# Hybrid RG-LRU / GLA step on one core: the first shift joined in behind the first projections, gates moved behind the second key, values' weights by column tiles

## The reference, cut to what matters

```python
mod = silu(c) @ ada_w + ada_b          # for each of the two conditions; six parts of 1024
shift1, scale1, gate1, shift2, scale2, gate2 = split(mod, 6)
h = rmsnorm(x, norm1_g) * (1 + scale1) + shift1
z = h @ w_in
xl, yl, q, k, v, og, gdn = split(z, (512, 512, 256, 256, 512, 512, 32))
xc = conv4(xl)                          # along the tokens, rows of 64 on the grid
# RG-LRU in both directions over xc, with gates from xc @ lru_wr, xc @ lru_wi (blocks of 64)
lru_out = gelu(yl) * (h_f + h_b)
glog = log_sigmoid(gdn @ gla_wg + gla_bg) / 16
# GLA in both directions, 4 heads, chunks of 64, cumulated glog in exponentials with q and k
x = x + gate1 * (concat(lru_out, norm(o) * silu(og)) @ w_out)
x = x + gate2 * moe(rmsnorm(x, norm2_g) * (1 + scale2) + shift2)     # 16 experts, 2 for each token
```

## Time and profile before

| what | value |
|---|---|
| median of 3 runs | 659.17 us (659.15 to 662.01) |
| profiled execution | 657.16 us, span 655.4 us |
| mean granted clock of TensorE | 0.943 |
| TensorE matmul busy | 572.9 us (87%) |
| VectorE, ScalarE, GpSimd busy | 242.9, 172.9, 51.4 us |
| moved by DMA | 131.42 MB, mean 201 GB/s |

### The profile page before, as it was taken

One profiled execution on the slowest core, in us unless ns is written; L12 is line 12 of the kernel. 1 busy time (PEld: TensorE's weight loads), 2 busy tenths in 40 slices (PEclk: granted clock), 3 DMA queues, 4 the chain that ended last, 5 costly groups with the idle time before them and its releaser, 6 DMA issues.

```text
span 655.4 us, 6115 instructions
## 1 busy us (share of the span) xinstructions
PE 572.9 (87%) x2354; PEld 304.5 (46%) x2354; DVE 242.9 (37%) x501; ACT 172.9 (26%) x314; POOL 51.4 (8%) x67
## 2 busy tenths in 40 slices
PE   2479989999969999999999999589999999999514
PEld 0145545544335556566545555535444454544201
DVE  0342438502951754111336665432112121211067
ACT  0630275638241220442311112010111101011122
POOL 3000000000060220000000000110001010100050
PEclk9789998999969999999999999588999999999957
DMA  9976245049533931500039000399999999972193
GB/s 326 392 241 193 61 148 205 1 133 348 192 128 81 358 89 40 176 1 1 1 109 392 31 14 33 121 378 341 382 365 368 372 359 381 352 265 96 66 343 137
DMA packets 76351, 131.42 MB, mean 201 GB/s; under 512 B 8137, under 2 KB 31010, under 8 KB 76322
## 3 DMA queue, kind: packets, MB, share of 16 engines
q1 hardware_dynamic: 70136, 108.96, 48.0%
q0 software_dynamic: 3744, 13.63, 5.5%
q10 hardware_dynamic: 2442, 8.43, 3.2%
HBM read 112.36 MB, written 18.65 MB: 200 GB/s over the span
## 4 chain that ended last, share of the span: by engine, by line
PE 55%; DVE 6%; ACT 2%; issue 1%; DMA 1%; POOL 1%; POOLq 0%; DVEq 0%; ACTq 0%
PE ms L1267 17%; PE ps L1201 11%; PE ps L1288 8%; PE ps L956 8%; PE ps L1250 2%; PE ps L1137 1%; PE ms L1172 1%; PE ps L1342 1%; DMA wring<-expert_rows,yidx 1%; PE ps L1127 1%; POOL wring L666 1%; PE ps L1086 1%; DVE tmp L1551 1%; PE ms L1240 1%; DVE tmp L1521 1%
## 5 line engine op out<-in xcount | busy, mean ns | idle before, releaser
L956 PE MATMUL ps<-r,wring 128*128 128x512 f32 (+1 forms) x512 | 143.9, 440 | 4.9 <-ACT gd L806 2.4
L956 PEld LDWEIGHTS ps<-r,wring 128*128 128x128 f32 x512 | 79.2, 192 | 69.1 <-issue 66.6
L1201 PE MATMUL ps<-wring,mixT 128*128 128x512 f32 x160 | 72.1, 599 | 0.5 <-DVE tmp L1640 0.5
L1267 PE MATMUL ms<-wring,tmp 128*128 128x512 f32 x128 | 58.8, 603 | 1.3 <-DVE tmp L1799 1.3
L1201 PEld LDWEIGHTS ps<-wring,mixT 128*128 128x128 f32 x160 | 29.2, 190 | 32.0 <-issue 31.3
L639 POOL DMA_INDIRECT mixT<-h_rows,slot_tok x16 | 15.3, 953 | 320.2 <-DVE slot_tok L1739 181.0
L1813 DVE COPY gd<-ps 128x256 f32<-128x256 f32 x16 | 6.8, 425 | 89.9 <-PE ps L1277 89.9
L972 PE MATMUL ps<-wring,cs 128*32 128x512 f32 x192 | 27.5, 719 | 12.9 <-DMA wring<-in_ada_w_dram 7.3
L904 ACT ACTIVATE tmp<-ms 128x256 f32<-128x256 f32 x16 | 6.1, 384 | 123.4 <-PE ms L1267 123.4
L1020 PE MATMUL ps<-wring,r 128*128 128x512 f32 x80 | 37.3, 623 | 1.4 <-ACT vtok L763 1.4
L1267 PEld LDWEIGHTS ms<-wring,tmp 128*128 128x128 f32 x128 | 24.2, 195 | 28.6 <-issue 27.0
(11 more groups left out here) (280 smaller groups left out, 716.6 us busy)
## 6 DMA issues: line engine op xcount, KB each, us to landing
wring<-in_ada_w_dram SPq DMA_DIRECT2D x12, 2048.0 KB, 12.9
wring<-in_exp_w_dram SPq DMA_DIRECT2D x8, 2048.0 KB, 13.6
r<-in_exp_w_dram SPq DMA_DIRECT2D x4, 2048.0 KB, 14.0
wring<-in_exp_w_dram SPq DMA_DIRECT2D x8, 1024.0 KB, 6.7
tmp<-in_exp_w_dram SPq DMA_DIRECT2D x4, 2048.0 KB, 14.3
expert_rows<-tmp ACTq DMA_DIRECT2D x16, 512.0 KB, 7.4
wring<-in_w_in_dram SPq DMA_DIRECT2D x12, 512.0 KB, 4.1
expert_rows<-zero SPq DMA_DIRECT2D x9, 512.0 KB
```

The costliest lines, as they stand in the source:

```text
L956: i = mm(d, lhsT, r, start=first, stop=last)
L1201: i = mm(product(f"mx{t}")[:, half * 512:(half + 1) * 512], mixT[:, k, t * P:(t + 1) * P], w[:, k, :], start=(k == 0), stop=(k == KD - 1))
L1267: i = mm(ms[:, b, :], xgT[:, b, k, :], e13[u % 4][:, k, :], start=(k == 0), stop=(k == KD - 1))
```

## The change

1. The first scales alone, from a2 and a3, now make `hT`; the shift is left out there. a2 and a3 and the xl weights are loaded ahead of a0 and a1, the small inputs and the rows of x ahead of all. The start's transposes stand among the products, and half of the scales (`first_scale`) is made from a2, half from a3.
2. a0 and a1 are multiplied behind xl0. Their sum with the bias is put into `shc` (128 x 8 x 32, in `gd`), a further product `adx` multiplies the xl weights with it, and its turned result `xb` is the bias that the shift brings to xl. ScalarE adds it to xl0 and xl1 in place (`bias_xl`) and to xl2 and xl3 as it takes them. Once xl3 is made, ScalarE and VectorE add the shift to `hT` in place (`shift_rows`), and gd waits for both.
3. The gates of chunks 2 and 3 stand right behind k1 and ahead of q0 on TensorE, and on ScalarE with their decays and roots ahead of the copies of q. Some turns and reductions of modulations stand later.
4. The weights of v are loaded in four tiles, each when the product of q or k that read those columns is made. a0 and a3 change slots, and so do the pieces behind them.

```diff
-        order = []
-        for j in range(4):
-            order += [(f"ad{j}", "A")] + [(f"aT{j - 1}", "D")] * (j > 0)
-        order += [("aT3", "D")]
-        order += [(f"xT{k}", "AD"[k % 2]) for k in range(KD)]
+        order = [("ad2", "A"), ("xT0", "A"), ("aT2", "D"), ("xT1", "D"), ("ad3", "A"), ("xT2", "A"), ("xT3", "D"), ("aT3", "D")]
+        order += [(f"xT{k}", "AD"[k % 2]) for k in range(4, KD)]
+        order += [("xl0", "A"), ("ad0", "A"), ("ad1", "A"), ("aT0", "D"), ("xl1", "A"), ("aT1", "D"), ("adx", "A"), ("xl2", "A"), ("aTx", "D")]
...
-        tiled = {"qk": ([f"xl{i}" for i in range(4)], 0), "og": (["v4"] * 4, 1), "yl": ([f"og{i}" for i in range(4)], 2)}
+        tiled = {"qk": (["adx", "adx", "xl2", "xl3"], 0), "v": (["q0", "q1", "k0", "k1"], 1), "og": (["v4"] * 4, 2),
+                 "yl": ([f"og{i}" for i in range(4)], 3)}
...
+            def bias_xl(t):
+                grid, rest = xl_parts(t)
+                act.wait_ge(took["A"], count(f"xl{t}")[1])
+                A(grid, grid, ACT.Identity, bias=xb[:, t, 0:1])
+                A(rest, rest, ACT.Identity, bias=xb[:, t, 1:2]).then_inc(xl_biased, 1)
+
+            def shift_rows():
+
+                act.wait_ge(shift_ready, 1)
+                act.wait_ge(product_ready, made["xl3"])
+                for k in range(0, KD, 2):
+                    A(hT[:, k, 0:NS], hT[:, k, 0:NS], ACT.Identity, bias=mod[:, k, 0:1])
+                    i = A(hT[:, k, NS:N], hT[:, k, NS:N], ACT.Identity, bias=mod[:, k, 1:2])
+                i.then_inc(hT_ready, 1)
...
             take_gates(1)
+            shift_rows()
+            take_mod(4)
+            take_mod(5)
             decays(0)
-            A(gd[:, :], ready("gd")[:, 0:N], ACT.Copy).then_inc(took["A"], 1)
...
             wait_piece(pe, "xl")
-            for t in range(3):
-                project(f"xl{t}", weights("xl"), t * P)
+            project("xl0", weights("xl"), 0)
+            two_of(modulation, 0)
+            project("xl1", weights("xl"), P, range(0, KD // 2))
+            two_of(turn_modulation, 0)
+            project("xl1", weights("xl"), P, range(KD // 2, KD))
+            modulation("x")
+            project("xl2", weights("xl"), 2 * P, range(0, KD // 2))
+            turn_modulation("x")
+            project("xl2", weights("xl"), 2 * P, range(KD // 2, KD))
...
             pe.wait_ge(gdw_in, 16)
+            pe.wait_ge(hT_ready, 2)
             dst = start("gd")
...
             project("k1", weights("qk"), QK + P)
+
+            for ch in (2, 3):
+                gates(ch, 0)
+                gates(ch, 1)
             wait_tile(pe, "qk", 0)
             project("q0", weights("qk"), 0)
             wait_tile(pe, "qk", 1)
             project("q1", weights("qk"), P)
             two_of(modulation, 6)
-            gates(2, 0)
+            for i in range(4):
+                wait_tile(pe, "v", i)
+            values(0)
             two_of(turn_modulation, 6)
-            gates(2, 1)
-            gates(3, 0)
-            gates(3, 1)
-            wait_piece(pe, "v")
-            values(0)
             values(1)
...
+            def first_scale(j):
+
+                a = 4 * (j - 2)
+                take_mod(j)
+                add_bias(KD + a, KD + a + 4)
+                for s in range(2):
+                    i = stt(A1[:, a:a + 4, s], mod[:, KD + a:KD + a + 4, s], 1.0, smT[:, N1 + a:N1 + a + 4], ALU.add, ALU.mult)
...
+            def shift_rows():
+                dve.wait_ge(product_ready, made["xl3"])
+                for k in range(1, KD, 2):
+                    ts_(hT[:, k, 0:NS], hT[:, k, 0:NS], mod[:, k, 0:1], None, ALU.add)
+                    i = ts_(hT[:, k, NS:N], hT[:, k, NS:N], mod[:, k, 1:2], None, ALU.add)
+                i.then_inc(hT_ready, 1)
...
             gate_input(1)
+            shift_rows()
+            recur(0)
             take_mod(4)
             take_mod(5)
-            recur(0)
             cumulate()
-            take_mod(6)
-            take_mod(7)
             gate_input(2)
```

More of the change, by code:

```diff
@@ L246, in turned @@
             return [(f"aT{j}", "D") for j in js]
-        order += [("xl0", "A"), ("xl1", "A"), ("xl2", "A")] + gates_order(0) + [("xl3", "A")] + gates_order(1)
-        order += adaln(4, 5) + [("gd", "A")] + turned(4, 5) + [("k0", "A")]
-        order += [(f"g{g}", "A") for g in range(4)] + [("k1", "A"), ("q0", "A")]
-        order += [("q1", "A")] + adaln(6, 7) + gates_order(2)[0:2] + turned(6, 7) + gates_order(2)[2:4] + gates_order(3)
-        order += [("v0", "A"), ("v1", "A")] + adaln(8, 9)
+        order += gates_order(0) + [("xl3", "A")] + gates_order(1)
+        order += adaln(4, 5) + [("gd", "A"), ("k0", "A")]
+        order += [(f"g{g}", "A") for g in range(4)] + turned(4, 5) + [("k1", "A")] + gates_order(2) + gates_order(3)
+        order += [("q0", "A"), ("q1", "A")] + adaln(6, 7)
+        order += [("v0", "A")] + turned(6, 7) + [("v1", "A")] + adaln(8, 9)
         order += [("v2", "A")] + turned(8, 9) + [("v3", "A")] + adaln(10, 11) + [("v4", "A")] + turned(10, 11)
@@ L268, in hybrid_step @@
                 made[name] = place[f"og{g}"] + n + 1
+        for n, name in enumerate(("aT0", "aT1", "xl1", "adx", "aTx", "xl2")):
+            made[name] = place["aT0"] + n + 1
         RING = 3
@@ L479, in _ @@
                                      blocks[half]).then_inc(lruw_in, 16)
+            load_piece("a4")
             load_piece("a5")
@@ L696, in take_mod @@
             def take_mod(j):
-                if j >= 2:
-                    act.wait_ge(product_ready, made[f"aT{j - 2}"])
-                A(adrow[j % 2], ready(f"ad{j}")[:, 0:512], ACT.Copy).then_inc(took["A"], 1)
-            take_mod(0)
-            take_mod(1)
+                n = modulations.index(j)
+                if n >= 2:
+                    act.wait_ge(product_ready, made[f"aT{modulations[n - 2]}"])
+                A(adrow[n % 2], ready(f"ad{j}")[:, 0:512], ACT.Copy).then_inc(took["A"], 1)
             for t in range(NT):
@@ L710, in _, with take_xT @@
             A(st[:, 2, :], st[:, 0, :], ACT.Sqrt, bias=eps[:, 0:1], scale=1 / D).then_inc(roots, 1)
+            def take_xT(k):
+                src = ready(f"xT{k}")
+                A(hT[:, k, 0:NS], src[:, 0:NS], ACT.Identity, bias=zero[:, 0:1], scale=A1[:, k, 0:1])
+                A(hT[:, k, NS:N], src[:, NS:N], ACT.Identity, bias=zero[:, 0:1], scale=A1[:, k, 1:2]).then_inc(took["A"], 1)
+            take_mod(2)
+            act.wait_ge(mod_out, 1)
+            take_xT(0)
+            take_mod(3)
+            take_xT(2)
+            act.wait_ge(mod_out, 2)
+            take_xT(4)
+            take_xT(6)
             chain(A(lam[:, 0, :], smT[:, LAM:LAM + 8], ACT.Abs))
@@ L986, in _, with turn_input @@
             pe.wait_ge(cs_ready, 1)
-            for j in range(4):
-                modulation(j)
-                if j:
-                    turn_modulation(j - 1)
-            turn_modulation(3)
-            pe.wait_ge(xhat_ready, 1)
-            for k in range(KD):
+            def turn_input(k):
+                pe.wait_ge(xhat_ready, 1)
                 dst = start(f"xT{k}")
@@ L997, in _ @@
                 i.then_inc(product_ready, 1)
+            modulation(2)
+            turn_input(0)
+            turn_modulation(2)
+            turn_input(1)
+            modulation(3)
+            turn_input(2)
+            turn_input(3)
+            turn_modulation(3)
+            for k in range(4, KD):
+                turn_input(k)
             wait_taken(pe, f"xT{KD - 1}")
```

152 lines of the change are left out of this document (98 added, 54 removed).

## The result

The changed kernel took **637.24 us** (median of 4, 635.88 to 639.00). The kernel before took 659.15, 659.17 and 662.01 us in the same comparison, and 796.21 in a fourth, disturbed execution that the ratio leaves out. The ratio is 0.9655 [0.9611, 0.9699], so the change made the kernel faster by 3.0 to 3.9% here; a second series of the same kernel, at the end of the experiments, gave 2.1 to 2.8%.

What follows compares the result with a forecast made beforehand. TensorE was taken as bound by an idle start chain, then 9.8 us of waits and 4.6 of slow clock; xl0 at 34.5 plus a 158.8 stage gives 193.3, 14.6 us earlier: 659.17 becomes 644.6 us, range 639.7 to 653.0.

Steps and rivals of the forecast that it cites:

- The start: Chain up to the first projection: xl0 starts at 34.5 us instead of 46.21, 11.7 us earlier.
- the short end: Start: xl0 at 33.1 us, if a2 lands by the rate alone and the transposes are warm.
- Full clock of the fourth product: Start, a3's product: after about 1.5 us idle it runs 1.8 us at full clock, against 3.5 at the low one.
- rival (a): The clock falls at each new wait; four products start low, 1.8 each, 7.2 us in all: 652; chance 0.15.
- The queue: Weight loads at the start: transfers of this queue land in the order of issue, at 388 GB/s.
- The stage: xl0 to the first attention transpose: 161.7 us before, less 9.8 waits and 4.6 clock, plus 6.95 work and 4.6 waits: 158.8.
- the new waits: TensorE in the stage: 0.9 before chunk 0's gates, 1.5 gd, 1.3 moved gates, 0.9 v0, 4.6 us together.
- the old waits: TensorE in the stage: 2.36 before k0, 0.70, 5.27 and 1.45 us go, 9.8 in all, with 4.6 of slow clock.
- Behind kT0: After the attention stage's first transpose at 207.92 us the programs are the same, so 447.5 us follow unchanged.
- The profile's offset: Whole time: the median of the runs, 659.17, lies 2.0 us above the profiled execution's 657.16; carried over, 642.6 becomes 644.6.
- (b): Gates wait for recurrence 1 or ScalarE: 3 us later, and the clock falls with it (1.8): 649; chance 0.10.
- (d): Slower: projections cut by small products and waits run long at low clock; all of xl0 to xl3 so gives 679; chance 0.03.

Runs made afterwards that it cites:

- the kernel with the gates alone: Kernel before with the gates of chunks 2 and 3 moved behind k1, start and load of v unchanged: 652.38 us, ratio 0.9909.
- the exchange with xl: Changed kernel with the weights of xl issued ahead of a2 and a3 in SP's queue: 642.64 us (one run).
- the gates late: Changed kernel with the gates of chunks 2 and 3 put back behind q1: 649.06 us, ratio 0.9849.
- The start alone: Changed kernel with the gates of chunks 2 and 3 back behind q1 and v loaded as one piece: 649.70 us, ratio 0.9868.

## Why the prediction was right and wrong

**The start, 34.5 forecast, 32.72 measured: mechanism right, size 1.8 too long.** Four small terms in front of the first scaling (25.1 forecast, 23.54 measured) make nearly all of it: a2's product was over at 21.2 and not at 22.1, since it started 0.5 earlier and took 3.27 us and not 3.6 (together 0.9); the turn of block 0 took 0.76 us and not 1.3, its five transposes being nearly at full clock (0.5); VectorE's reduction to ScalarE's scaling was 0.76 and not 0.95 (0.2). Block 0 was then taken in 1.18 us (1.2), a3's product took 1.92 (1.8), and the rest up to xl0 6.1 (6.4). Warm transposes and the earlier landing had been listed as the short end, 33.1; the longer values were taken. Of the 6.4 us the named terms give 6.25 before any turn of x is counted, so that sum was partly a guess; 6.1 was measured.

**Full clock of the fourth product: right.** The wait was 1.51 as forecast and the product took 1.92. This wait, the 0.98, 0.71 and 1.10 us in the changed kernel did not bring a low clock, and rival (a) did not come in the stage. The premise, that 1.22 and 2.36 us bracket it, was weaker than it looked: the same wait of 2.36 us left the clock full in the kernel with the gates alone, and in the attention the clock fell with no wait over 0.9 us. So part of this success is luck. The Trainium skill ("TensorE: Matmul & The Clock Gate", HAM oscillation) tells of a kernel in which every burst of products behind a long wait for a transfer begins at the low clock. The runs agree for their long ones: behind 4.57 and 5.67 us the product of values took 9.95 and 9.74 us for 7.11.

**The queue: right.** Pieces land in the order of issue, as the exchange with xl showed: 2.1 MB put ahead moved a2's product by 5.16 us.

**The stage, 158.8 forecast, 157.4 measured: the new waits were over-priced.** They were put at 4.6 us and were 2.66: gates of chunk 0 0.71 (0.9, though its own terms, 5.1 less 4.34, give 0.76), gd 0.98 (1.5), moved gates 0.54 (1.3), v0 0.43 (0.9). ScalarE's shift took 0.91 a block as bounded (3.7 with its overlap, 4.1 taken), VectorE's 0.59 (2.45, 2.6 taken). Of the moved gates the half that waits for recurrence 1 was nothing: VectorE's reduction was done 23.0 us behind gd's product (23.4 forecast), just when k1's was (22.8 forecast). The other half, for the bank behind k1's copy and the table load, was 0.54 (0.7). The other terms of the stage, work and clock, were 0.5 us off the other way. That the old waits go was right, and the runs show by what: with the gates late three of them came back (0.71, 5.26 and 1.44 us, with their slow clock); the fourth, 2.36 us before k0, stood in the kernel with the gates moved alone and in none with the shift joined in.

**What each part is worth.** kT0 moved 17.8 us. The start alone gave 6.4 of it (13.0 in the start, less 6.6 of joined-in work and waits in the stage), the gates and tiles on top the other 11.4. Alone the gates are worth 3.1 us in the stage, alone the tiles 0.3; the tiles under the moved gates 7.9. They can't be added up one by one.

**Behind kT0: the step that failed.** "655.4 - 207.92 = 447.5 us follow", taken as unchanged because the programs are. The work is unchanged, its clock isn't. In eleven profiles TensorE's idle time behind kT0 was 46.8 to 47.8 us whatever the kernel, and its busy time with the same 1625 products 396.0 to 404.0: 400.0, 400.4, 397.8 in the three with the program of before there, and 397.2, 400.6, 396.3, 397.7, 400.2, 397.4, 396.0 and 404.0 in eight with that of after. The changed kernel's 2.9 us came from there, by no mechanism of the change that any run found. The tail is a term of the sum with a spread of its own, 443.4 to 451.1 us, and had been given none. Without these 2.9 us the result would have been 640.1, inside the range.

Whether the change brings the shorter tail about or only met it stays open. Among 52 undisturbed executions of the kernel before, none took less than 656.07 us (span 654.3; with kT0 at 207.8 that leaves 446.5 for the tail), so the tails of 443.4 and 444.5 of the changed kernel were never met there. The gates alone, with the program of before behind kT0, had 445.6. So what TensorE did earlier may well shift the stretches of low clock in the same way each time. No run tests that rival.

**The profile's offset.** 2.0 us between the profiled execution and the median of three were carried over; in the changed kernel it was 0.7, and the larger series of the kernel before have medians of 657.24 to 659.73, so the offset too was a matter of which executions had been met. With 1.8 (start), 1.4 (stage) and 2.9 (tail) that makes the 7.4 us by which the forecast was too high.

**The rivals.** (b) didn't come: the moved gates waited 0.54 us in all. (d) neither: no low clock between xl0 and kT0.

**The range** held the ends of the steps, and no end of it held a faster tail; 2.5 us were missing, less than that tail. The second series of the changed kernel, at 642.86, lies inside it, 14.8 us under the kernel before on that chip, against the 14.6 forecast. That is luck and no confirmation: its first group gained 17.1 us up to kT0 by the profile, and what the others lost again goes with a lower clock (0.955), of which the forecast had nothing.

## What to carry to other kernels

A reordering and a finer load can be worth little each and much together: look whether the wait that one removes is covered by the other, and price them as a pair. A stretch "behind the change" whose program is the same still gets an uncertainty of its own where its TensorE clock is below full in places; take it from the spread of the executions, not from one profile. And a gain under a few microseconds is to be read from the start of a named instruction, or from the distance between two, in several profiles; the whole time can hide it, and the first projection alone came at 32.6 to 33.8 us in seven profiles of one start.

## What the hardware showed that was not expected

- In the attention the granted clock fell in two kernels (0.69 and 0.62 in windows of one), behind waits of 0.89 and 0.45 us, and not in another with the same waits; it stayed at 1.00 behind waits of 1.51 and 1.10 us in the start.
- Behind the same wait of 2.36 us the same 32 products took 10.58, 10.58 and 10.57 us in three profiles and 8.89 in a fourth.
- Executions of one program on one chip came in two groups, 635 to 636 us at a mean clock of 0.967 and 642 to 643 at 0.955.
- Filling waits with products that compute nothing raised the clock there (20 products in 2.38 us instead of 4.43), and the next products gained nothing by it (the clock was 0.50 from 405.6 to 408.6 us, and the expert's 16 took 8.00 us, where 7.90 had been).
- The first large product of the changed kernel, behind 11 us of idle, took 3.27 us (up to 3.64 in other runs) for what takes 1.92 shortly after, and the granted clock is recorded as 1.00 there.
- The products of values could start 4.07 us after the product that freed the slot of their last 128 columns (512 KB), so that load had landed by then; with one piece of 2 MB it took 9.3.
